# Weight-block sums of the u and gate groups made by adding transfers, with their products spread over more chunks

## The reference

```python
h = rmsnorm(x, a_norm)
z = h @ w_in                            # (256, 2048) @ (2048, 12288)
u, v, gate = jnp.split(z, 3, axis=-1)   # each (256, 4096)
u = gelu(u); v = rmsnorm(gelu(v), v_gain)
sv = einsum('gpq,bnqgc->bnpgc', w_s, v in 8 groups) + b_s
x = x + (u * sv * silu(gate)) @ w_out
```

## Time and profile before

| | us |
|---|---|
| median of three runs | 2096.27 (2093.90 to 2096.86) |
| the profiled execution | 2095.56 |
| its span | 2093.8 |
| TensorE busy | 2081.4 (99%) |
| VectorE busy | 1575.8 (75%) |
| ScalarE busy | 1143.4 (55%) |
| GpSimd busy | 37.5 (2%) |

### The profile page before, as it was taken

One profiled execution on the slowest core, in us unless ns is written; L12 is line 12 of the kernel. 1 busy time (PEld: TensorE's weight loads), 2 busy tenths in 40 slices (PEclk: granted clock), 3 DMA queues, 4 the chain that ended last, 5 costly groups with the idle time before them and its releaser, 6 DMA issues.

```text
span 2093.8 us, 25361 instructions
## 1 busy us (share of the span) xinstructions
PE 2081.4 (99%) x9952; PEld 1741.4 (83%) x9952; DVE 1575.8 (75%) x1774; ACT 1143.4 (55%) x1354; POOL 37.5 (2%) x41
## 2 busy tenths in 40 slices
PE   9999999999999999999999999999999999999999
PEld 7887888888888887888888888888888888888887
DVE  7988787877897754655669678867777777779986
ACT  6766555555556544555455454555555555555553
POOL 0000000000000000100000000000000000000000
PEclk9999999999999999999999999999999999999999
DMA  8657777777764555544465656555555556556663
GB/s 337 211 197 215 216 232 221 216 233 212 285 224 151 198 192 169 181 152 156 149 209 180 221 171 210 162 186 193 184 186 196 181 192 190 182 179 234 225 203 134
DMA packets 115415, 417.00 MB, mean 199 GB/s; under 512 B 12896, under 2 KB 13664, under 8 KB 114784
## 3 DMA queue, kind: packets, MB, share of 16 engines
q1 hardware_dynamic: 109440, 394.66, 56.3%
q0 software_dynamic: 3456, 12.58, 3.6%
q10 hardware_dynamic: 2400, 8.14, 1.1%
HBM read 413.23 MB, written 2.10 MB: 198 GB/s over the span
## 4 chain that ended last, share of the span: by engine, by line
PE 86%; DVE 7%; ACT 3%; issue 2%; DMA 2%; ACTq 0%; DVEq 0%
PE g L736 29%; PE g L633 21%; PE xs L658 8%; PE g L658 8%; PE xs L759 7%; PE xs L662 4%; PE g L662 4%; PE g L763 4%; DVE w_lo L1548 3%; ACT w_hi L1101 2%; DMA raw<-in_stream 1%; PE xs L681 1%; PE xs L918 0%; DMA ge_block<-in_stream 0%; DVE t L1735 0%
## 5 line engine op out<-in xcount | busy, mean ns | idle before, releaser
L1548 DVE TENSOR_TENSOR w_lo<-raw,w_hi 128x1024 fp32r<-128x1024 f32 x643 | 783.1, 1222 | 398.5 <-ACT w_hi L1101 390.2
L1101 ACT ACTIVATE w_hi<-raw 128x1024 fp32r<-128x1024 f32 x643 | 680.1, 1059 | 660.8 <-PE g L633 222.1
L736 PE MATMUL g<-w_hi,in_both 128*128 128x512 f32 x1120 | 355.9, 390 | 1.2 <-DVE w_lo L1619 0.7
L633 PE MATMUL g<-w_hi,mid_both 128*128 128x512 f32 x1024 | 326.7, 394 | 0.0
L736 PEld LDWEIGHTS g<-w_hi,in_both 128*128 128x128 f32 x1120 | 210.2, 188 | 47.0 <-DVE w_lo L1548 1.3
L633 PEld LDWEIGHTS g<-w_hi,mid_both 128*128 128x128 f32 x1024 | 192.3, 188 | 39.6
L736 PE MATMUL g<-w_lo,in_both 128*128 128x512 f32 x560 | 217.9, 389 | 0.0
L633 PE MATMUL g<-w_lo,mid_both 128*128 128x512 f32 x512 | 199.4, 389 | 0.0
L658 PE MATMUL g<-mlp_both,w_hi 128*128 128x512 f32 x704 | 176.8, 393 | 0.0
L658 PE MATMUL xs<-mlp_both,w_hi 128*128 128x512 f32 x704 | 176.3, 392 | 0.0
L658 PEld LDWEIGHTS g<-mlp_both,w_hi 128*128 128x128 f32 x704 | 126.6, 189 | 22.8
(11 more groups left out here) (440 smaller groups left out, 3182.5 us busy)
## 6 DMA issues: line engine op xcount, KB each, us to landing
raw<-in_stream SPq DMA_DIRECT2D x643, 512.0 KB, 4.0
d_block<-in_stream SPq DMA_DIRECT2D x28, 512.0 KB, 4.5
o_block<-in_stream SPq DMA_DIRECT2D x24, 512.0 KB, 4.6
v_block<-in_stream SPq DMA_DIRECT2D x20, 512.0 KB, 4.2
ge_block<-in_stream POOLq DMA_DIRECT2D x15, 512.0 KB, 5.5
gm_block<-in_stream SPq DMA_DIRECT2D x12, 512.0 KB, 5.2
ge_block<-in_stream SPq DMA_DIRECT2D x10, 512.0 KB, 4.4
gl_block<-in_stream POOLq DMA_DIRECT2D x6, 512.0 KB, 5.5
```

The lines of the kernel that those rows point to most:

```text
L633: ins = mm(G[buf][:, t, :], a[:, kt, at_t], w[:, slot, j * COLS:(j + 1) * COLS], start=(kt == 0 and n == 0), stop=(last and j == ROWS_PER_ ...
L736: ins = mm(GG[:, bank, :], a[:, kt, t * P:(t + 1) * P], w[:, slot, half_chunk(j)], start=n == 0 and opens(item, bank), stop=ended and n == ...
L1101: activation(w_hi[:, n % RING, :], of[:], ACT.Copy).then_inc(hi_ready, 1)
L1548: v.tensor_tensor(w_lo[:, n % RING, :], of, w_hi[:, n % RING, :].bitcast(F32), ALU.subtract).then_inc(lo_ready, 1)
```

## The change

The sum for product 5 is an adding DMA too: GpSimd issues it when product 1's block has been split. The one for product 7 no longer waits for it and is issued as soon as B12 is loaded. VectorE makes no block sum in the ug phase. In the order of a group the products stand further apart: product 1 moves from item 4 to 5, product 5 from 6 to 8, product 6 from 11 to 12. In group 0 the spatial product follows item 15 instead of 14, and what belongs to it moves by one item. The final norm's row and half of the residual are loaded in the last ug group, at items 2 and 9, the other half at the start of out1. The row sums of out1 are made at items 2 and 6.

```diff
--- before.py
+++ after.py
@@ -99,16 +99,16 @@
 SUM_TURNS = {"v": (3, 2), "out1": (4, 5), "down": (0, 1, 2, 6), "gm0": (3, 2), "out2": (1,)}
 
 
-SUMS_AT = {"v": (4, 8), "out1": (1, 4), "down": (3, 6, 9, 64), "gm0": (-8, -5), "out2": (-7,)}
+SUMS_AT = {"v": (4, 8), "out1": (2, 6), "down": (3, 6, 9, 64), "gm0": (-8, -5), "out2": (-7,)}
 
 
 
 
 UG_TURN = 2
-UG_FIRST = ((0, "C0"), (0, "C1"), 1, (0, "C2"), 5, (0, "C3"), (1, "C0"), (1, "C1"), 7, 6, (1, "C2"), (1, "C3"),
+UG_FIRST = ((0, "C0"), 1, (0, "C1"), (0, "C2"), (0, "C3"), 5, (1, "C0"), 7, (1, "C1"), 6, (1, "C2"), (1, "C3"),
             3, 2, 4, (3, "C0"), (3, "C1"), (3, "C2"), (3, "C3"))
-UG_ORDER = ((0, "C0"), (0, "C1"), (0, "C2"), (0, "C3"), 1, (1, "C0"), 5, (1, "C1"), (1, "C2"), (1, "C3"), 7, 6,
-            (3, "C0"), (3, "C1"), 3, 2, 4, (3, "C2"), (3, "C3"))
+UG_ORDER = ((0, "C0"), (0, "C1"), (0, "C2"), (0, "C3"), (1, "C0"), 1, (1, "C1"), (1, "C2"), 5, (1, "C3"), 7,
+            (3, "C0"), 6, (3, "C1"), 3, 2, 4, (3, "C2"), (3, "C3"))
 UG_ITEMS = len(UG_ORDER)
 UG_HALF_ENDS = (16, 18)
 WIDE = tuple(WIDE_STEPS) + ("ug",)
@@ -237,7 +237,7 @@
 def sums_made(q, p):
 
 
-    ahead = sum(1 if phase == "ug" else 4 for phase, _, _ in QUADS[:q])
+    ahead = sum(0 if phase == "ug" else 4 for phase, _, _ in QUADS[:q])
     return ahead + {5: 1, 7: 2, 6: 3, 4: 4}[p]
 
 
@@ -805,7 +805,7 @@
                 pe.wait_ge(lo_ready, at_item + 1)
                 step = wide_product if item.product else wide_chunk
                 step(item, norm_in.hi, norm_in.lo, at_item % RING).then_inc(mm_done, 1)
-                if k == (0 if i else 14):
+                if k == (0 if i else 15):
                     spatial(i)
                 if i and k == 3:
                     y_turned(i - 1)
@@ -1087,7 +1087,7 @@
                     of = wide(item.phase, item.group).blocks[buffer_of(q, b)]
                     if item.product in (1, 3, 2):
                         act.wait_ge(block_full[b], 16 * loads_of_block(q, b))
-                    elif item.phase == "ug" and item.product != 5:
+                    elif item.phase == "ug":
                         act.wait_ge(sem[f"block_added{item.product}"], 16 * (item.group + 1))
                     else:
                         act.wait_ge(sem["block_sums"], sums_made(q, item.product))
@@ -1300,10 +1300,14 @@
                     ws_high(0)
                 if i and k == 3:
                     y_high(i - 1)
-                if k == (5 if i else 15) and i + 1 < GROUPS:
+                if k == (5 if i else 16) and i + 1 < GROUPS:
                     v_high(i + 1)
-                if k == (6 if i else 15) and i + 1 < GROUPS:
+                if k == (6 if i else 16) and i + 1 < GROUPS:
                     ws_high(i + 1)
+                if i == GROUPS - 1 and k == 2:
+                    act.dma_start(final_row[:], final_rows).then_inc(sem["final_in"], 16)
+                if i == GROUPS - 1 and k == 9:
+                    act.dma_start(xt[:, 1, :], x_tokens[:, 1, :]).then_inc(sem["x_again"], 16)
                 first_product("ug", FIRST_ITEM["ug"] + n)
                 if k == UG_HALF_ENDS[0]:
                     u_gelu(i)
@@ -1327,8 +1331,7 @@
                 split("out1", n)
                 if n == 0:
                     act.wait_ge(lo_ready, FIRST_ITEM["out1"])
-                    act.dma_start(xt[:], x_tokens).then_inc(sem["x_again"], 16)
-                    act.dma_start(final_row[:], final_rows).then_inc(sem["final_in"], 16)
+                    act.dma_start(xt[:, 0, :], x_tokens[:, 0, :]).then_inc(sem["x_again"], 16)
                 sums_high("out1", n)
                 if n == 4:
                     y_high(GROUPS - 1)
@@ -1555,15 +1558,15 @@
             def block_sums(n):
 
                 item, before = ITEMS[n], ITEMS[n - 1]
+                if item.phase == "ug":
+
+                    return
                 if item.product == 1:
                     q = quad_of(item)
                     dve.wait_ge(block_full[B11], 16 * loads_of_block(q, B11))
                     dve.wait_ge(block_full[B12], 16 * loads_of_block(q, B12))
                     dve.wait_ge(lo_ready, n + 1)
                     block_sum(item, B11, B12, B11)
-                elif item.phase == "ug":
-
-                    return
                 elif before.product == 1:
                     q = quad_of(before)
                     dve.wait_ge(block_full[B22], 16 * loads_of_block(q, B22))
@@ -1795,16 +1798,16 @@
                 if i and k == 0:
                     gate_times(i - 1)
                     y_product(i - 1)
-                if k == (1 if i else 15):
+                if k == (1 if i else 16):
                     sv_gained(i)
                 if i and k == 4:
                     y_low(i - 1)
-                if k == (6 if i else 16) and i + 1 < GROUPS:
+                if k == (6 if i else 17) and i + 1 < GROUPS:
                     low(v_lo[:, i + 1], v_all[:, i + 1], v_hi[:], "v_hi_ready", i + 2, "v_lo_ready")
                 if k == (7 if i else 17) and i + 1 < GROUPS:
                     ws_low(i + 1)
                 ug_own_products(i, k)
-                if k == 17:
+                if k == (17 if i else 18):
                     u_times(i)
 
             def added(phase, q, of):
@@ -1866,7 +1869,7 @@
                 if n == 5:
                     y_low(GROUPS - 1)
                 if at_item == product_item("out1", 0, 5, 6) - 1:
-                    dve.wait_ge(sem["x_again"], 16)
+                    dve.wait_ge(sem["x_again"], 32)
                 add_products("out1", at_item, xt)
                 if n in (out1_second + 2, out1_second + 5):
                     gained_low(norm_mid, (n - out1_second - 2) // 3, 0, TR)
@@ -2217,12 +2220,14 @@
                 if item.phase != "ug" or item.product not in (1, 5, 6):
                     return
                 q, g = quad_of(item), item.group
-                product, to, b = {1: (7, B12, B22), 5: (6, B11, B22), 6: (4, B11, B21)}[item.product]
+                product, b = {1: (5, B12), 5: (6, B22), 6: (4, B21)}[item.product]
                 if item.product == 1:
-                    pool.wait_ge(sem["block_sums"], sums_made(q, 5))
-                else:
-                    pool.wait_ge(lo_ready, n + 1)
-                p.dma_start(wide("ug", g).blocks[to][:], stream[block_row(q, b)], accum_op=ALU.add).then_inc(
+
+                    pool.wait_ge(block_full[B12], 16 * loads_of_block(q, B12))
+                    p.dma_start(wide("ug", g).blocks[B12][:], stream[block_row(q, B22)],
+                                accum_op=ALU.add).then_inc(sem["block_added7"], 16)
+                pool.wait_ge(lo_ready, n + 1)
+                p.dma_start(wide("ug", g).blocks[B11][:], stream[block_row(q, b)], accum_op=ALU.add).then_inc(
                     sem[f"block_added{product}"], 16)
 
             pool.wait_ge(sem["minus_half_ready"], 1)
```

## The result

The changed kernel takes 2105.23 us (median of four runs, 2104.39 to 2108.61) against 2095.22 for the kernel before beside it: ratio 1.0054, 95% interval 1.0041 to 1.0067. It is slower, and outside the range given. The profiled execution is the slowest of the four: it took 2108.61 us, span 2106.7, 13.05 more than the one of before.

A forecast was written before the change was run, and what follows sets the result against it. TensorE was taken as the bound, with a loop of splits and adding transfers binding lightly beside it. Terms -6.2 + 3.4 + 2.5 = -0.3 us gave 2095.3 us, range 2089.5 to 2102.5.

The forecast's parts named there:

- What goes (-6.2): TensorE's waits removed: gain product -2.8 us, group 0's last own-product read -2.0, out1's weight split -1.4.
- The loop: Splits and adding transfers for products 5, 6, 4: 45.4 us a round, 0.74 too long per group, +3.4 us seen by TensorE.
- the sum of 6.1 and 14.65: Loop's VectorE part: 6.1 us from product 4's split to the u result, 14.65 from there to product 1's split.
- 28.9 + L5 + L6 + L4: Loop's round trip in us, predicted as 28.9 + 3L; L is an adding transfer's time from issue to landing.
- I take 5.5: Landing time of each of the loop's three adding transfers: median 5.5 us, at least 5.2, up to 9.0.
- rival C: Same loop with transfer engines at 85%, mean landing 5.75 us and both early loads hitting group 7: +6.5, 2102.1 us; chance 0.25.
- Group 7: a size: Two early 1 MB loads in the last ug group delay the loop's transfers: +2.5 us, bounds 0 and 4.1.
- 0.3 us of slack: Amount subtracted from rival C's loop cost; the slack at the loop's start was worked out as 1.05 us.
- raw chunks behind the fourth transfer: Raw chunks may wait behind each group's added transfer: 0 to 2.4 us a group, nothing taken.
- The rule on queue rows taking turns: Transfer engines alternate between queue rows by whole packets, so early loads' cost in group 7 stays between 0 and 4.1 us.
- The lock of the shared port: GpSimd's 32 transfer issues could each be held while VectorE has the shared port; the trace was taken to speak against it.

The follow-up runs named there:

- experiment 12: Changed kernel with only the gain row's load issued five items later in each group; 2098.10 us, ratio 1.0019 to the kernel before.
- loads back: Changed kernel with the final norm's row and both halves of the residual loaded at the start of out1 again; 2103.64 us, ratio 1.0046.
- old order: As a run: kernel before with all four block sums by adding transfers, its item order, loads and row sums kept; 2095.11 us, ratio 0.9999.
- experiments 5 and 6: Each against the changed kernel: 5 (split first), VectorE's gate and y products after item 5's split, 2096.82 us; 6 (product 1 at item 4), that move alone, 2098.87 us.
- 7 late: Changed kernel with product 7's adding transfer issued after product 5's instead of before it; 2102.35 us, ratio 1.0044.
- no transfer for 7: Changed kernel without product 7's adding transfer, so B22 is not added and the output is not the reference's; 2104.13 us, ratio 1.0042.
- loads cleared: Changed kernel with the next B12 loaded at product 4 and the gain row five items later; 2097.60 us, ratio 1.0014.
- new order and VectorE's sum: Changed kernel with product 5's sum on VectorE again and product 7's transfer behind it; 2097.90 us, ratio 1.0017.
- experiments 7 and 8: Changed kernel with its new order in group 0 alone: 7 with residual and final row loaded at out1, 2088.58 us; 8 with the early loads, 2086.99 us.

## Why the prediction was wrong

**What goes (-6.2): right in kind, a little more in size.** Both kinds of wait in the ug phase are gone, group 0 is 2.66 us shorter (2.0 was taken), out1 1.7 (1.4). An undisturbed group takes 44.42 us, not the 44.66 taken, since a start after a wait costs some 0.25 us beyond the wait shown; so 0.66 per group could be won instead of the wait alone. The ug phase of 361.5 us has 6.9 to lose against eight undisturbed groups (354.6); with out1's 1.7 that makes 8.6.

**The loop: right, and its length too.** From the end of product 4's split (305.22) to that of product 1's (325.94) are 20.72 us in the changed kernel; the sum of 6.1 and 14.65 said 20.75. With the landings that the trace has, 28.9 + L5 + L6 + L4 gives 45.6, 48.5, 45.6, 48.1, 48.2 and 46.9 us for the rounds from group 1 to group 7; from one issue of product 5's transfer to the next the trace has 46.4, 48.2, 45.4, 47.9, 47.9 and 46.6.

**The step that failed: "I take 5.5, since in each group the three transfers start with at most a chunk and the block loads in front of them, as before."** For products 5 and 6 it held (5.35 and 5.39 in the mean of groups 1 to 6). For product 4 it was 7.53. A mean of 18.3 for the three gives rounds of 47.2 us, 2.8 over the 44.42 of an undisturbed group, where the prediction had 0.74. This was rival C's mechanism: C took 5.75 in the mean, the trace has 6.1. Why product 4's transfer is late is known in part: without the gain row in front it lands after 6.17 (experiment 12). The rest is open.

**Group 7: a size.** 2.5 was taken for the two early loads, bounds 0 and 4.1. Landings were 7.3 for product 5 and 9.2 for product 4, against 5.4 and 5.7 with the loads back: 5.4 in the loop. This is from one execution each; in the trace of experiment 12 the same two loads are there and the landings are 5.3 and 6.3.

**The clock: not in the sum, and little in the time.** The changed kernel's ug phase (376.2) exceeds eight undisturbed groups (354.6) by 21.6 us. The first wait, in group 2, makes 2.95 of it. From the end of product 4's split in group 2 (305.22) to that in group 7 (543.35) are 238.13 us, 16.0 more than five times 44.42. Two stretches at half clock lie in between, but the loop does not feel them: from product 4's split to product 1's are 20.72 us in group 3, behind which the clock stays full, and 20.72 in groups 2 and 4, where it falls. TensorE loses 1.7 us each time and then waits so much less for the loop. Only the stretch behind the last wait of group 7, where no further round of the loop hides it, is lost on top, 2.7 us. In the prediction's terms: 8.6 gone, 13.5 for the loop and its start, 5.4 for group 7's loads, 2.7 for the clock, 13.0 in all, where the profiled execution has 13.05. One more execution says the same: at a mean granted clock of 1.000 it took 2104.78 us, 9.6 over the kernel before.

**What the loop was not compared with: the old order.** Moving product 1 from item 4 to item 5 had put gate and y products in front of its split, 3.72 us. The prediction counted them in the loop's length and did not ask whether the old order had them there too; in the old order the same four transfers have some 2 us to spare in each round (42.4 against 44.42). A rival "the order, not the transfer" was missing among those given. How the rest of the cost divides between that place and the shorter distances, experiments 5 and 6 bound but do not settle.

Two smaller things. Rival C's sum takes off 0.3 us of slack where the working before it has 1.05. And raw chunks behind the fourth transfer, for which nothing was taken, did not stop TensorE: in groups 1 to 6 its waits of over 0.3 us are all on product 4's split.

The rule on queue rows taking turns (the Trainium skill, "DMA: Bandwidth & Descriptors", section "Queues, rings and completion order") was said to leave the two early loads between 0 and 4.1 us; the trace has 5.4, and no run here separates turns between rows from plain waiting behind what came first. The lock of the shared port (the Trainium skill, "SBUF — State Buffer", section "SBUF: two separate sides") did not show. The Trainium skill ties that warning to VectorE instructions in a mode that uses two ports, a condition that the prediction left out; in the changed kernel the issues for products 5, 6 and 4 in groups 1 to 7 take 0.86 us each, as before.

## What to carry to other kernels

When a step on a compute engine becomes a transfer, write down the closed round (split, transfer, split, ..., back to the first split) with every instruction that stands in front of the first one, compare it with the period, and do the same for the order before: the same four transfers gave +10 us in one order of a group's items and, with a better first group, -8 us in the other. Price a transfer in a loop by its late landings, not by its median: of three transfers two kept to it, and the third decided the time. Before a time at reduced clock is added to a sum, ask whether TensorE is what the next wait hangs on: inside a loop that other engines close, the same microseconds come off the next wait. And a transfer is a cheap way of making a sum only where the next order keeps slack for a late one: in the old order landings up to 6.6 us cost nothing.

## What the runs showed of the hardware

After some waits TensorE's clock is granted at half, 1.2 GHz. Idle stretches of TensorE in the ug phase and what followed: 2.70 and 2.31 us (changed kernel), 2.59 (loads back), 2.82 (7 late), 3.14 (old order), 3.27 (split first), 3.53 (product 1 at item 4), 3.17, 2.40 and 1.85 (no transfer for 7): 3.4 us at half clock each; 3.56 (changed, group 7) and 4.00 (loads cleared): 6.8 us. Waits of 1.61 us and less did not do it, nor did 2.38 in the kernel before, 2.40 with the new order and VectorE's sum, and 2.86 in group 7 without the transfer for 7. Part of such a stretch can lie inside the wait itself. So TensorE lost 1.5 to 1.7 us beyond a wait of 1.85 to 3.53 that was followed by half clock, and 2.7 and 3.0 beyond the two longer ones.

What tells 2.40 with a fall from 2.86 without one is open. That executions of one kernel differ in it is on record: of 77 executions of the kernel before, 22 show a mean clock of 0.999 and take 2094.9 to 2098.5 us, and the others show 1.000 and take 2092.5 to 2095.2. A mean of 0.999 is what one stretch of 3.4 us at half clock makes; the profiled execution is of the second kind, so where it lies in the first is not shown. The two kernels of experiments 7 and 8, which have no such wait, show 1.000 in all 11 executions; the 5 of experiment 8 lie within 0.3 us of each other.

Also open is what exactly holds product 4's transfer. Moving the loads in front of it helps, but with both moved single landings of 6.7 and 7.3 remain, and with the same loads in front the old order has 5.6 to 6.6 in groups 1 to 6.
